# A hybrid decoder step: x normed anew for tiles 2 and 3, evictions on ACT, and the GDN's first mask on its decay

## The reference

```python
h = rmsnorm(x, norm_w)
proj = einsum('bld,de->ble', h, w_in)
xbc_in, dt_raw, qkv_in, b_raw, a_raw, q_mem, z = split(proj)
xbc = silu(causal_conv(xbc_in))              # Mamba-2 SSD group, 16 heads
qkv = silu(causal_conv(qkv_in))              # gated DeltaNet (GDN) group, 8 heads
Amat = where(strict, (kb @ k.T) * decay, 0)  # GDN, decay = exp of differences of sums
T = inverse(eye + Amat)
y_mem = softmax(q_mem @ mem_k.T) @ mem_v     # 4 heads, 256 memory tokens
y = concat(headnorm(y_ssd), headnorm(y_gdn), headnorm(y_mem)) * mix_norm_w * silu(z)
out = rmsnorm(x + y @ w_out, final_norm_w)
```

## Time and profile before

| | |
|---|---|
| median of three runs | 1467.01 us |
| the profiled execution | 1462.25 us |
| its span, first to last instruction | 1460.1 us |
| mean granted clock of TensorE | 0.978 |
| busy: PE, DVE, ACT, POOL | 1330.4, 788.4, 611.7, 444.9 us |
| busy share of PE | 91% |

### The profile page before, as it was taken

How to read it: one execution, slowest core, us unless ns; L and a number is a source line. 1 busy time by engine, 2 the same in 40 slices (tenths; PEclk the granted TensorE clock), 3 DMA queues, 4 the chain that set the end, 5 groups by cost and what they waited for, 6 DMA issues and landing times.

```text
span 1460.1 us, 26074 instructions
## 1 busy us (share of the span) xinstructions
PE 1330.4 (91%) x10569; PEld 1281.0 (88%) x10569; DVE 788.4 (54%) x1345; ACT 611.7 (42%) x1186; POOL 444.9 (30%) x457
## 2 busy tenths in 40 slices
PE   6789989899999899898989989999999799997995
PEld 6789989779888889888888889999989799997995
DVE  6763345422666354746657483534354757665554
ACT  7463346422434253524343533334352543344553
POOL 0520010103444354535444452635340312112112
PEclk9989999999999899999999999999999999999998
DMA  8134442262111213231423122222222266666662
GB/s 306 43 102 130 144 160 58 62 188 80 48 45 49 67 59 104 73 102 48 144 60 102 60 88 60 73 61 73 74 59 64 74 242 205 225 221 199 189 180 100
DMA packets 48406, 161.26 MB, mean 110 GB/s; under 512 B 5296, under 2 KB 10832, under 8 KB 48032
## 3 DMA queue, kind: packets, MB, share of 16 engines
q1 hardware_dynamic: 39344, 130.77, 29.3%
q10 hardware_dynamic: 8832, 28.33, 5.5%
q0 software_dynamic: 112, 0.50, 0.1%
HBM read 144.32 MB, written 15.26 MB: 109 GB/s over the span
## 4 chain that ended last, share of the span: by engine, by line
PE 72%; DVE 11%; ACT 7%; issue 5%; POOL 1%; DMA 1%; SPq 1%; ACTq 1%; DVEq 0%; POOLq 0%
PE ps L873 36%; PE ps L1175 15%; PE ps L772 11%; DVE s_st L1953 2%; PE ps L829 2%; PE ps L833 2%; DVE d_junk L1962 1%; PE ps L1143 1%; PE ps L1125 1%; ACT w_hi L1205 1%; ACT g_e L1386 1%; DVE fin L2060 1%; DMA w_raw<-in_w_in 1%; DVE g_p L1875 1%; DVE conv_a L1759 1%
## 5 line engine op out<-in xcount | busy, mean ns | idle before, releaser
L873 PE MATMUL ps<-h_hi,w_hi 128*128 128x260 f32 x1888 | 414.9, 302 | 39.5 <-issue 21.0
L873 PE MATMUL ps<-h_lo,w_hi 128*128 128x260 f32 x1888 | 384.2, 285 | 0.0
L873 PE MATMUL ps<-h_hi,w_lo 128*128 128x260 f32 x1888 | 383.8, 285 | 0.0
L1205 ACT ACTIVATE w_hi<-w_raw 128x512 fp32r<-128x512 f32 x428 | 256.4, 624 | 288.0 <-PE ps L873 137.6
L873 PEld LDWEIGHTS ps<-h_hi,w_hi 128*128 128x128 f32 x1888 | 296.6, 193 | 52.8 <-issue 43.4
L2072 POOL TENSOR_TENSOR w_lo<-w_raw,w_hi 128x512 fp32r<-128x512 f32 x156 | 209.8, 1353 | 311.6 <-ACT w_hi L1205 311.4
L873 PEld LDWEIGHTS ps<-h_lo,w_hi 128*128 128x128 f32 x1888 | 296.7, 192 | 0.0
L873 PEld LDWEIGHTS ps<-h_hi,w_lo 128*128 128x128 f32 x1888 | 295.6, 191 | 0.0
L1591 DVE TENSOR_TENSOR w_lo<-w_raw,w_hi 128x512 fp32r<-128x512 f32 x272 | 187.0, 711 | 143.6 <-ACT w_hi L1205 141.8
L1175 PE MATMUL ps<-y_hi,w_hi 128*128 128x260 f32 x640 | 185.2, 289 | 12.7 <-issue 4.9
L1175 PE MATMUL ps<-y_lo,w_hi 128*128 128x260 f32 x640 | 183.2, 286 | 0.0
(11 more groups left out here) (366 smaller groups left out, 1924.2 us busy)
## 6 DMA issues: line engine op xcount, KB each, us to landing
w_raw<-in_w_in SPq DMA_DIRECT2D x120, 512.0 KB, 3.6
w_raw<-in_w_out SPq DMA_DIRECT2D x80, 512.0 KB, 4.2
w_raw<-in_w_mem SPq DMA_DIRECT2D x16, 512.0 KB, 3.6
x_t<-in_x_t SPq DMA_DIRECT2D x8, 520.0 KB, 9.6
fin<-in_x_t SPq DMA_DIRECT2D x8, 520.0 KB, 5.7
out_y_t<-fin SPq DMA_DIRECT2D x16, 260.0 KB, 2.3
c_kv<-in_c_k ACTq DMA_DIRECT2D x8, 512.0 KB, 6.0
c_kv<-in_c_v ACTq DMA_DIRECT2D x8, 512.0 KB, 4.2
```

The costliest lines, as they stand in the source:

```text
L873: last = mm(out[:, hf, :], w, a[:, kk, HALF * hf:HALF * hf + HALF], start=(kk == 0 and j == 0), stop=(kk == KT - 1 and j == 2))
L1205: A(w_hi_of(g)[:, s], raw[:, g % NRAW, s], ACT.Copy).then_inc(sem("w_hi_done"), 1)
```

## The change

Tiles 0 and 1 are as before, except that block 0 of x is split before unit 1's weights and units 2 and 3 are split behind blocks 5 and 7. For all later tiles h_hi and h_lo are made a second time, from x times norm_w times x_rstd ("xn", block by block, x_w in the place of conv_a), each block as soon as small has read it, and tiles 2 and 3 run block by block beside this. The later tiles need no factor when they leave PSUM, and ACT empties them: a conv tile by two ACTIVATEs (a copy to conv_u and the last tap to conv_a), a q_mem tile by copies, a z tile by Silu from PSUM; their post steps come one place earlier. The history products, all of tile 0's and 1's post but the eviction, and tile 2's post stand behind tiles 2 and 3. The memory's squares are made by ACT and summed by 16 products with ones on TensorE. The small steps stand among tiles 4 and 5, the kv units among tiles 6 and 7, four after each half tile. The copy of x_rstd for late tiles ("rstdmove") goes. Units 6 and 7 use the place of units 2 and 3. In GDN GpSimd multiplies g_e1 with level 0's mask into g_p, VectorE makes g_p = -Gram x g_p and then natf, and the turn of it goes to PSUM bank side[2] instead of side[0]. csts and w_small are loaded behind units 3 and 4, masks and the second half of mem behind the last x_w.

```diff
-    items = [("const",), ("xunit", 0), ("xunit", 1)]
+    items = [("const",), ("xunit", 0), ("xh", 0), ("xunit", 1)]
     for k in range(KT):
-        items += [("xh", k)] + [("xunit", k - 2)] * (k in (4, 5)) + [("proj", 0, k), ("proj", 1, k)]
-    items += [("xrstd",), ("setup",), ("small",)] + [("post", 0, s) for s in range(6)]
-
+        items += [("xh", k)] * (k > 0) + [("xunit", 2)] * (k == 5) + [("xunit", 3)] * (k == 7) + [("proj", 0, k), ("proj", 1, k)]
+    items += [("xrstd",), ("setup",), ("small",), ("xunit", 4), ("xunit", 5), ("post", 0, 0), ("post", 1, 0)]
+    for k in range(KT):
+        items += [("xn", k)] + [("xunit", 6)] * (k == 5) + [("xunit", 7)] * (k == 7) + [("proj", 2, k), ("proj", 3, k)]
+    items += [("xend",)]
+    for n in range(2):
+        items += [("post", n, s) for s in range(1, 7)]
+    items += [("post", 2, s) for s in range(6)]
+
+    msq = [("msq", k) for k in range(KT)]
     mh = [("mh", k) for k in range(KT)]
-    early = [("msq",), ("smallturn",), PAUSE, PAUSE, ("smallpost",)] + mh[:5] + [("smallpost2",)] + mh[5:9] + [("smallcum",)]
-    early += mh[9:11] + [("smallend",)] + mh[11:13] + [("mrstd",)] + mh[13:15] + [PAUSE, ("mcol",), mh[15]]
-    items += spread(proj_items(2, EARLY_SSD), early)
-
-    for it in proj_items(EARLY_SSD, T_KV):
+    early = [("smallturn",), PAUSE, PAUSE, ("smallpost",)] + msq[:8] + [("smallpost2",), PAUSE, PAUSE, ("smallexp",)] + msq[8:12]
+    early += [("smallcum",)] + msq[12:14] + [("smallend",)] + msq[14:] + [("mrstd",)] + mh[:2] + [PAUSE, ("mcol",)] + mh[2:6]
+    items += spread(proj_items(EARLY_SSD, T_MEM), early)
+
+    for it in proj_items(T_MEM, T_KV):
         items.append(it)
         if it[0] == "proj" and it[2] % 8 == 7:
-            u = 4 * (it[1] - EARLY_SSD) + it[2] // 8 * 2
-            items += [("kv", u), ("kv", u + 1)]
+            for u in range(4 * (2 * (it[1] - T_MEM) + it[2] // 8), 4 * (2 * (it[1] - T_MEM) + it[2] // 8) + 4):
+                items += mh[u + 6:u + 7] + [("kv", u)]
...
-            main.insert(main.index(("proj", first, KT - 2)), ("rstdmove",))
...
-    items += [("post", NTILE - 1, s) for s in range(4)] + [("yhi", Y_ORDER[-1]), ("ylo", Y_ORDER[-1])]
+    items += [("post", NTILE - 1, s) for s in range(3)] + [("yhi", Y_ORDER[-1]), ("ylo", Y_ORDER[-1])]
...
+        if g in (2, 3, 6, 7):
+            return w_first[g % 2][0][:, :]
...
+    def tile_out(n):
+
+        if n < 2:
+            return sem("first_read"), n + 1
+        return sem("tile_read"), n - 1
...
+            elif k == "msq":
+                kk = it[1]
+                if kk == 0:
+                    pe.wait_ge(*upto("small_copied", 1))
+                pe.wait_ge(*upto("m_sq", kk + 1))
+                mm(side[1][:, 0:MEM_T], ones, m_sq[:, kk % 2, :], start=kk == 0, stop=kk == KT - 1).then_inc(sem("m_sq_used"), 1)
...
+                pe.wait_ge(*upto("m_hi", kk + 1))
+                pe.wait_ge(*upto("m_lo", kk + 1))
                 if kk == 0:
-                    pe.wait_ge(*upto("m_hi", KT))
-                    pe.wait_ge(*upto("m_lo", KT))
...
+                if n in (0, 2):
+                    pe.wait_ge(*upto("x_hi", KT * (n // 2) + kk + 1))
+                    pe.wait_ge(*upto("x_lo", KT * (n // 2) + kk + 1))
                 if kk == 0 and n >= 2:
-                    pe.wait_ge(*upto("tile_read", n - 1))
+                    pe.wait_ge(*tile_out(n - 2))
...
-                    pe.wait_ge(*upto("g_natm", 7 * h + 1))
+                    pe.wait_ge(*upto("g_nat0", h + 1))
                     for c in range(NC):
-                        last = one(quad(side[0])[:, c, :], g_natm[0][:, c, :], ident_r[:, :])
+                        last = one(quad(side[2])[:, c, :], g_p[:, c, :], ident_r[:, :])
...
+                A(m_col[:, 0:1], eps[:, 0:1], ACT.Copy)
...
+            elif k == "xn":
+                kk = it[1]
+                act.wait_ge(*upto("small_ps", kk + 1))
+                act.wait_ge(*upto("x_w", kk + 1))
+                A(h_hi[:, kk, :], x_w[:, kk % 2, :], ACT.Copy).then_inc(sem("x_hi"), 1)
+            elif k == "msq":
+                kk = it[1]
...
+                if kk >= 2:
+                    act.wait_ge(*upto("m_sq_used", kk - 1))
+                A(m_sq[:, kk % 2, :], mem_t[:, kk, :] if kk < 8 else mem_t2[:, kk - 8, :], ACT.Square).then_inc(sem("m_sq"), 1)
...
+                if s == 0 and n >= 2:
+                    act.wait_ge(*upto("unit_used", tile_units(n)))
...
+                    if s == 1 and n < 2:
+                        act.wait_ge(*tile_out(n))
+                        act.wait_ge(*upto("x_lo", 2 * KT))
+                        A(conv_a[:, b, :], conv_u[:, b, :], ACT.Identity, scale=conv_w[:, ci, 3:4], bias=bias).then_inc(sem("conv_id"), 1)
+                    if s == 0 and n >= 2:
                         conv_before, z_before = before_in_buf(n, ("ssd", "gdn")), before_in_buf(n, ("z",))
+                        act.wait_ge(*upto("tap_done", 4 * (conv_at[conv_before] + 1)))
+                        act.wait_ge(*upto("tail_done", 2 * (conv_at[conv_before] + 1)))
+                        act.wait_ge(*upto("conv_out", conv_at[conv_before] + 1))
...
+                        A(halves(conv_u[:, b, :]), proj_ps(n), ACT.Copy).then_inc(sem("conv_u"), 1)
+                        A(halves(conv_a[:, b, :]), proj_ps(n), ACT.Identity, scale=conv_w[:, ci, 3:4], bias=bias).then_inc(sem("tile_read"), 1)
...
-                elif kind == "z" and s == 1:
+                elif kind == "qm":
+                    if s == 0:
+                        A(halves(y_raw[:, 16 + i, :]), proj_ps(n), ACT.Copy)
+                        A(dec[:, NCONV + i, :], proj_ps(n)[:, 0, 0:DB], ACT.Copy).then_inc(sem("tile_read"), 1)
...
+                    A(halves(conv_a[:, b, :]), proj_ps(n), ACT.Silu).then_inc(sem("tile_read"), 1)
...
+            elif k == "xn":
+                kk = it[1]
+                if kk == 0:
+                    dve.wait_ge(*upto("x_ss", 1))
+                    dve.wait_ge(*upto("rstd", 1))
+                else:
+                    dve.wait_ge(*upto("x_lo", KT + kk - 1)) if kk > 1 else None
+                V.scalar_tensor_tensor(x_w[:, kk % 2, :], x_t[:, kk, :], norm_w[:, kk:kk + 1], x_rstd[:, :], ALU.mult, ALU.mult).then_inc(sem("x_w"), 1)
+                for k2 in ([kk - 1] if kk else []) + ([kk] if kk == KT - 1 else []):
+                    dve.wait_ge(*upto("x_hi", KT + k2 + 1))
+                    V.tensor_tensor(h_lo[:, k2, :], x_w[:, k2 % 2, :], h_hi[:, k2, :].bitcast(F32), ALU.subtract).then_inc(sem("x_lo"), 1)
...
-                    dve.wait_ge(*upto("g_exp", 2 * h + 1))
+                    dve.wait_ge(*upto("g_mask0", h + 1))
+                    V.scalar_tensor_tensor(flat4(g_p), side[0], -1.0, flat4(g_p).bitcast(F32), ALU.mult, ALU.mult).then_inc(sem("g_nat0"), 1)
                     V.scalar_tensor_tensor(flat4(g_natf), side[0], -1.0, flat4(g_e1), ALU.mult, ALU.mult).then_inc(sem("g_nat"), 1)
+                    dve.wait_ge(*upto("g_nat0", h + 1))
+                    V.tensor_tensor(g_tt[:, :, :], g_p[:, :, :].bitcast(F32), across(ident, NC), ALU.add).then_inc(sem("g_tt0"), 1)
                     dve.wait_ge(*upto("g_exp", 2 * h + 2))
                     V.tensor_tensor(g_attn[:, :, :], quad(side[1]), g_e2[:, :, :], ALU.mult).then_inc(sem("g_attn"), 1)
                 elif s == 3:
-
-                    dve.wait_ge(*upto("g_natm", 7 * h + 1))
-                    V.tensor_tensor(g_tt[:, :, :], g_natm[0][:, :, :].bitcast(F32), across(ident, NC), ALU.add).then_inc(sem("g_tt0"), 1)
                     dve.wait_ge(*upto("g_t0_ps", h + 1))
-                    V.tensor_tensor(g_t[:, :, :], quad(side[0]), across(ident, NC), ALU.add).then_inc(sem("g_t_new"), 1)
+                    V.tensor_tensor(g_t[:, :, :], quad(side[2]), across(ident, NC), ALU.add).then_inc(sem("g_t_new"), 1)
...
-            if k == "msq":
-                pool.wait_ge(*upto("small_ps", 1))
-                for kk in range(KT):
-                    pool.wait_ge(*upto("mem_in" if kk < 8 else "mem2_in", 16))
-                    src = mem_t[:, kk, :] if kk < 8 else mem_t2[:, kk - 8, :]
...
+                    else:
+                        pool.wait_ge(*upto("g_tat", 6 * h))
+                    pool.wait_ge(*upto("g_exp", 2 * h + 1))
+                    G.tensor_tensor(g_p[:, :, :], g_e1[:, :, :], across(masks[:, 0, :], NC), ALU.mult).then_inc(sem("g_mask0"), 1)
                     pool.wait_ge(*upto("g_nat", h + 1))
-                for level in (0, 1) if s == 2 else (s // 2,):
+                for level in (1,) if s == 2 else (s // 2,):
                     if level == 1:
                         pool.wait_ge(*upto("g_attn", h + 1))
                     elif level == 2:
-                        pool.wait_ge(*upto("g_t0_ps", h + 1))
-                        pool.wait_ge(*upto("g_tt0", h + 1))
+                        pool.wait_ge(*upto("g_nat", h + 1))
```

(22 more changed lines are left out.)

142 lines of the change are left out of this document (49 added, 93 removed).

## The result

The changed kernel takes 1474.64 us in the median (1470.66 to 1476.11, 15 runs), the kernel before 1466.52 us in as many runs beside it: a ratio of 1.0047 (95% interval 1.0035 to 1.0059), so 0.47% slower. I had forecast 1461.0, and faster. The profiled execution took 1473.2 us with a span of 1471.0; before it was 1462.25 and 1460.1, so the traces differ by 10.9 us where the medians differ by 8.1: the profiled execution of before was one of its shorter ones. Over all timings of this document two executions stand far apart, 4539 us of the kernel before and 2618 us of run b2; they enter no ratio.

A forecast was written before the change was run, and what follows sets the result against it. Bound by TensorE except one hole and 43.5 us of waits in the heads; +4.9 front, 0 attention, -1.5 SSD, -8.4 GDN, -1 projections' end give -6.0: 1456.3 profiled, 1461 median, range 1449 to 1475.

The forecast's parts named there:

- the GDN term: GDN heads: z tile's Silu straight from PSUM shortens the chain, 1.5 us in heads 0 to 4, 0.3 in 5 to 7: -8.4.
- The moved mask is not what pays: GDN heads: with the mask on the decay the chain keeps the same length, since Exp comes last, not Gram.
- My +3: GDN heads, slower bound for all heads: ACT's double eviction ahead of a g_tt copy, 0.7 more than the Identity alone.
- a sign of being wrong: Forecast wrong if the hole is under 5 or over 14 us, or heads 1 to 4 don't get shorter.
- Start: Kernel start to the end of tiles 0 and 1: ends at 35.0 instead of 39.37, -4.4 us (bounds -1 and -6.5).
- tiles 2 and 3: Block-by-block tiles beside x's new norming, 1.38 us a block on VectorE: end at 72.4 instead of 91.9.
- hole: TensorE idle ahead of tile 4 until ACT empties tile 2: 9.6 us, to 81.9 (bounds 7 and 14), replacing 12.35.
- tiles 4 to 7: Memory projection stretch: 91.0 us plus clock 2.1, small work 1.1, squares 6.9, waits 4.7 gives 105.8, ending 187.8.
- The squares: Tiles 4 to 7: summing mem's squares on TensorE takes 16 products of 0.43, 6.9 us.
- Attention: Attention stage: VectorE loses a product, ACT gains a copy per conv tile: change 0 (bounds -3 and +4).
- SSD: SSD stage: TensorE's waits on VectorE steps, s_l first, shrink: -1.5 us (bounds -5 and +2).
- The slow one: Rival: squares and hole cost more, TensorE idle over 29 us from 35 us to kv's end: 1476, chance 0.21.

The follow-up runs named there:

- b2: The kernel after with VectorE's history products moved from "xend" back to the setup step, ahead of tiles 2 and 3: ratio 1.0043 to before.
- a1: The kernel after with GDN's old mask path (level 0's masked matrix made by GpSimd, turn from side bank 0): 1462.55 us, ratio 0.9949 to before.
- a2: The kernel before with only GDN's new mask path added, the front as before: ratio 1.0065 to before.
- a3: The kernel after with GpSimd's level-1 mask issued one step of the head later, behind the weight splits: 1462.47 us, ratio 0.9956 to before.
- d4: The kernel after with two VectorE operations exchanged in each head, g_attn ahead of g_tt0: ratio 1.0019 to before.
- c1: a1 with z tiles emptied by VectorE's copy again and ACT's Silu made in SBUF one step later: ratio 1.0010 to before.
- a5: The kernel after with the memory's squares still made by ACT but summed by VectorE, one TensorE product left: 1469.67 us, ratio 1.0019 to before.

## Why the prediction was wrong

**The step that failed** is the GDN term, by its sentences on the mask: "The moved mask is not what pays", "the same length", and "level 1's mask now waits for attn and ends at 681.5, so level 1 is issued 0.7 earlier". I had the order right, followed the mask to its own product on TensorE, and stopped. Queued behind the waiting mask on GpSimd were the low halves of the next weights, which the projection blocks between the heads' steps need, and there was no slack. It cost 10 to 14 us where I had 0: a1 and a2 show that it is the mask path, a3 and d4 that it is GpSimd's stand with the splits behind it. My +3 as the upper bound for all heads was a bound of the wrong thing: I had bounded only ACT's double emptying.

**What I put beside it was right.** The z tile's Silu and the emptying by ACT were to bring 8.4; they brought 7.8 to 8.0 by the traces (a1 against before, after against a2) and 7.5 to 12.4 by the timings, 5.9 or 9 of it for z (c1). The place is right too: from before to a1 the head lengths 0 to 4 shrink by 8.6 us together (I had 7.5) and the next two grow by 0.6. In the kernel after, the two terms nearly cancel in heads 1 to 4, where I had looked for a sign of being wrong: they are 1.2 us shorter together, with head 3 longer by 1.5. Heads 0, 5 and 6 grow by 2.2, 1.6 and 3.9. On the mask alone "the same length" is not far off either: with the queue's effect gone (a3), the new path is 1.6 us longer than a1's in seven head lengths, within the scatter.

**The clock's share** was missing from the term: I took idle time in the heads at its face. 8.3 us of waits came with 6.1 us of slower matmuls (6.8 with 3.8 by the means).

**Start** -4.8 (predicted -4.4), **tiles 2 and 3** ending at 72.44 (72.4), **hole** 9.19 us to 81.63 (9.6, to 81.9), **tiles 4 to 7** 106.2 (105.8) and the end of the keys 187.8 (187.8), both to the prediction's mark: right, from the order of the lists and the durations of the earlier trace rows. Within tiles 4 to 7 two errors cancel, which is luck. My waits were too long: 2.4 us for 4.7 (the first square 1.3 for 3.4, none at the small turns or smallexp, but 1.0 at the memory's scale). And TensorE was busy 103.8 us against 91.0 + 6.9 + 1.1 = 99.0 by my terms, 4.8 more where I had 2.1 for the clock. About 3.7 of it is the clock (an estimate from its 6.3 busy us at 0.50 from 80 to 88 us and 2.7 at a mean of 0.80 from 88 to 92); the rest is open. **The squares** at 16 x 0.43 were sized well (a5: 5.4 back of 6.5, with a new wait of 3.0).

**Attention** +1.0 (0) and **SSD** -0.3 (-1.5): the extra copy per conv tile on ACT (0.60, predicted 0.7) may have cost about what VectorE's lost product gave; no run separates the two.

**The rivals.** The slow one ended where the time ended, near 1475, but by another mechanism: TensorE's idle time from 35 us to the keys' end was 13.5, far under its point of 29. None of my cases had the slowdown in the heads. What I had from the Trainium skill (SBUF — State Buffer, section Who interferes with whom), that the early mask would hold up g_qg's product, did not come: the product takes 0.69 in six of the eight heads and 1.83 in heads 5 and 6. There the trace agrees with the rule, but the GpSimd instruction is another: the product began at 920.88 together with a weight split of 1.28 us, and the mask only at 922.13. VectorE then waited 1.13 us for the mask, so this hardly counted.
